# Differential attention: meta rows as one unit, the first softmax's divisor on the outputs, score halves issued alternately

## The chip, the cores and the metric

The kernel runs on one core of one Trainium2 chip. The metric is the device time of one execution in microseconds (us). A core has TensorE (PE, with its weight loads PEld), VectorE (DVE), ScalarE (ACT), GpSimd (POOL) and the queue of SyncE (SP), which work side by side and wait for each other by semaphores. PSUM is the memory that TensorE writes, in 8 banks of 512 fp32 columns.

## The reference, cut to what matters

One encoder layer on two request groups (G = 2) of 512 tokens, each with the same 16 learned meta tokens in front, so T = 528 rows per group. The change touches differential attention alone: 4 heads, each with two halves j of 64 query and key columns and 128 value columns.

```python
def _diff_attention(q, k, v, lam):            # q, k: (B, H, 2, L, 64)
    s = jnp.einsum('bhjqd,bhjkd->bhjqk', qblk, k).astype(jnp.float32)
    p = jax.nn.softmax(s, axis=-1)
    a = p[:, :, 0] - lam * p[:, :, 1]
    return jnp.einsum('bhqk,bhkd->bhqd', a.astype(v.dtype), v)

oa = _diff_attention(dq, dk, dv, lam)
oa = _rmsnorm(oa, g_da_out) * (1.0 - lam_init)   # over the 128 columns of a head
```

Ahead of it stand an RMSNorm and one projection (q, k, v and the mLSTM's inputs); after it the mLSTM, the output projection and 16 experts of expert-choice SwiGLU.

## The kernel before

The program is a row of stages, each a block in which every engine runs its own list: `project`, `attention`, `mlstm`, `project_out`, `experts`. Attention (L677) begins about 400 us into the span and ends at 589.

It works in units (g, c, h): a group, one of five row tiles c (tile 0 holds the 16 meta rows, tiles 1 to 4 hold 128 rows each) and a head, 2 x 5 x 4 = 40 in this order, g outermost. Keys are 528 columns. Meta rows see the keys of their own group, so they are computed once for each group, as 4 units of 16 rows each. The steps of a unit:

- `scores` (L766, TensorE): for each half j, q times k in a split of fp32 into high and low parts (high x high, high x low, low x high), each in two pieces of 264 columns: 12 matmuls, 64 rows deep. Half 0 goes to PSUM banks 0 and 1, half 1 to banks 2 and 3; each half waits for the exponential of the same half of the unit before (`s_exp`), which reads those banks.
- `maxima` (L930, VectorE): the negated maximum of each row and half, from PSUM.
- `softmax` (L831, ScalarE): exp(score - maximum) and its row sum, for each half.
- `combine` (L937, VectorE): the reciprocals of both sums, the second times -lambda, then a = p0 / l0 (L947) and a += p1 x (-lambda / l1) (L948), both 128 x 528.
- `turn` (L782, TensorE) and `read_turned` (L841, ScalarE): a is transposed in five pieces into banks 4 and 5 and copied to SBUF.
- `values` (L793, TensorE): a times v into the head's quarter of bank 6. The first head of a tile waits for `o_read`, that the bank of the tile before has been read.

Four heads make a tile of outputs: `read_out` (L851, ScalarE) copies bank 6 to `osb` (L856) and squares it (L858), `sum_out` (L951, VectorE) adds the squares, `rstd_out` takes the reciprocal root, `norm_out` (L746, POOL) scales by it and by the gain, `turn_out` (L807, TensorE) transposes into bank 7, `store_out` (L865, ScalarE) writes `mixT`.

The order is written out by hand: every engine runs a loop over s, and what it does in turn s is:

```python
# TensorE                                # VectorE
if s < N: scores(s)                      if s < N: maxima(s)
if 2 <= s <= N + 1: turn(s - 2)          if r == 0: sum_out(t)
if 3 <= s <= N + 2: values(s - 3)        if 1 <= s <= N: combine(s - 1)
```

ScalarE's turn s is `store_out` and `read_out` (one turn in four), `rstd_out` (one in four), `softmax(s)`, `read_turned(s - 2)`. In the first turns the engines also split q and k of the next head (`high_qk` on ScalarE, L872 and L873; `low_q` on VectorE, L960; POOL the low part of k, L758), and from turn 4 on, with one step in each of turns 8 to 15, VectorE computes the mLSTM's gate rows (L904 to L927).

Of the kernel before, what the change touches and what calls it, by code (L numbers as in the profile page):

```python
# [676 lines left out]
def attention(nc, e):  # L677
# [13 lines left out]
    rcp = tiles("rcp", [P, 2, 2])  # L691
    so = tiles("so", [P, HEADS])

# [10 lines left out]
    gt_loaded, g_abs, g_exp, l_ready = sem("gt_loaded"), sem("g_abs"), sem("g_exp"), sem("l_ready")  # L704
# [5 lines left out]
    units = [(g, c, h) for g in range(G) for c in range(NC5) for h in range(HEADS)]  # L710
    N = len(units)


    LAST = N + 8

    with nc.Block() as block:

        @block.sync
        def _(sp):
# [9 lines left out]
            load_rows(V, 0, v_loaded)  # L729
            for k in range(4):  # L730
# [12 lines left out]
        def _(pool):  # L743
            step = chained(pool, pool_step)

            def norm_out(t):  # L746
                R = CROWS[t % NC5]
# [3 lines left out]
                o, y = (x[0:R, :].rearrange("p (h d) -> p h d", h=HEADS) for x in (osb, on))  # L751
                step(nc.gpsimd.tensor_tensor(y, o, so[0:R, :].unsqueeze(2).to_broadcast([R, HEADS, HD]), ALU.mult))
                nc.gpsimd.tensor_tensor(y, y, gda[0:R, :].unsqueeze(1).to_broadcast([R, HEADS, HD]),
                                        ALU.mult).then_inc(on_ready, 1)
# [4 lines left out]
            for t in range(G * NC5):  # L759
                norm_out(t)  # L760
# [4 lines left out]
        def _(pe):  # L765
            def scores(i):  # L766
                g, c, h = units[i]
                R, a = CROWS[c], ZCOL[zc(g, c)]
                if i < HEADS:
                    pe.wait_ge(q_low, h + 1)  # L770
                    pe.wait_ge(k_low, h + 1)
                for j in range(2):
                    if i >= 1:
                        pe.wait_ge(s_exp, 2 * (i - 1) + j + 1)
                    for i3, (q, k) in enumerate(((q_hi, k_hi), (q_hi, k_lo), (q_lo, k_hi))):
                        for at, b, end in HALVES:
                            mm = pe.matmul(banks(2 * j, R)[:, at:at + end - b], q[QD * j:QD * j + QD, h, a:a + R],
                                           k[QD * j:QD * j + QD, h, SEQ * g + b:SEQ * g + end], start=(i3 == 0),
                                           stop=(i3 == 2))
                    mm.then_inc(s_done, 1)  # L780

            def turn(i):  # L782
                g, c, _ = units[i]
                R = CROWS[c]
# [3 lines left out]
                for k in range(NC5):  # L788
                    n, b = CROWS[(k + 1) % NC5], kcol(zc(g, (k + 1) % NC5)) - SEQ * g
                    mm = pe.transpose(banks(4, n)[:, k * P:k * P + R], diff[i % 2][0:R, b:b + n], ident[0:R, 0:R])  # L790
                mm.then_inc(aT_done, 1)

            def values(i):  # L793
                g, c, h = units[i]
                R = CROWS[c]
                pe.wait_ge(aT_read, i + 1)
                if c == 0 and h == 0:
                    pe.wait_ge(v_loaded[g], 32 if g == 0 else 16)
                if h == 0 and i > 0:
                    pe.wait_ge(o_read, i // 4)  # L800
                for k in range(NC5):
                    n = P if k < 4 else N_META
                    mm = pe.matmul(banks(6, R)[:, h * HD:(h + 1) * HD], diffT[i % 2][0:n, k, 0:R],
                                   V[0:n, zc(g, (k + 1) % NC5), h * HD:(h + 1) * HD], start=(k == 0), stop=(k == 4))
                mm.then_inc(pv_done, 1)

            def turn_out(t):  # L807
                R = CROWS[t % NC5]
                pe.wait_ge(on_ready, t + 1)
                if t >= 1:  # L810
                    pe.wait_ge(oT_read, t)
                for h in range(HEADS):
                    mm = pe.transpose(banks(7)[:, h * P:h * P + R], on[0:R, h * HD:(h + 1) * HD], ident[0:R, 0:R])
                mm.then_inc(oT_done, 1)

            for s in range(LAST):
# [4 lines left out]
                if 3 <= s <= N + 2:  # L821
                    values(s - 3)
                if s >= 10 and s % 4 == 2 and (s - 10) // 4 < G * NC5:
                    turn_out((s - 10) // 4)

        @block.scalar
        def _(act):
# [3 lines left out]
            def softmax(i):  # L831
                R = CROWS[units[i][1]]
                for j in range(2):
                    act.wait_ge(s_max, 2 * i + j + 1)
                    if i >= 2:
                        act.wait_ge(a_ready, i - 1)
                    nc.scalar.activation(prob[i % 2][j][0:R, :], banks(2 * j, R)[:, PH:PH + T], ACT.Exp,
                                         bias=nmax[0:R, i % 2, j:j + 1],
                                         accum_out=lsum[0:R, i % 2, j:j + 1]).then_inc(s_exp, 1)

            def read_turned(i):  # L841
                R = CROWS[units[i][1]]
                act.wait_ge(aT_done, i + 1)
                if i >= 2:
                    act.wait_ge(pv_done, i - 1)
                src = banks(4)[:, 0:4 * P].rearrange("p (k t) -> p k t", k=4)[:, :, 0:R]
                nc.scalar.activation(diffT[i % 2][:, 0:4, 0:R], src, ACT.Copy)
                nc.scalar.activation(diffT[i % 2][0:N_META, 4, 0:R], banks(5, N_META)[:, 0:R],
                                     ACT.Copy).then_inc(aT_read, 1)

            def read_out(t):  # L851
                R = CROWS[t % NC5]
                act.wait_ge(pv_done, 4 * t + 4)
                if t >= 1:
                    act.wait_ge(on_ready, t)
                nc.scalar.activation(osb[0:R, :], banks(6, R)[:, 0:HALF], ACT.Copy).then_inc(o_read, 1)  # L856
                act.wait_ge(o_read, t + 1)
                nc.scalar.activation(osq[0:R, :], osb[0:R, :], ACT.Square).then_inc(osq_ready, 1)  # L858

            def rstd_out(t):  # L860
                R = CROWS[t % NC5]
                act.wait_ge(so_ready, t + 1)
                rms_rstd(nc, step, so[0:R, :], so[0:R, :], HD, eps[0:R, :]).then_inc(or_ready, 1)

            def store_out(t):  # L865
                R, a = CROWS[t % NC5], mixcol(*divmod(t, NC5))
                act.wait_ge(oT_done, t + 1)
                src = banks(7)[:, 0:HALF].rearrange("p (h t) -> p h t", h=HEADS)[:, :, 0:R]
                nc.scalar.activation(mixT[:, 0:HEADS, a:a + R], src, ACT.Copy).then_inc(oT_read, 1)
# [4 lines left out]

            high_qk(0)
            high_qk(1)
            for s in range(LAST + 2):
                t, r = divmod(s - 7, 4)
                if r == 0 and 0 <= t - 1 < G * NC5:
                    store_out(t - 1)  # L880
                if r == 0 and 0 <= t < G * NC5:
                    read_out(t)
                if r == 1 and 0 <= t < G * NC5:
                    rstd_out(t)
                if 2 <= s + 1 < HEADS:
                    high_qk(s + 1)
                if s < N:
                    softmax(s)
                if 2 <= s <= N + 1:
                    read_turned(s - 2)  # L890
                if s == 5:
# [3 lines left out]
                    nc.scalar.activation(ga[:], ga[:], ACT.Ln, bias=1.0).then_inc(g_exp, 1)  # L895

        @block.vector
        def _(dve):
# [31 lines left out]
            def maxima(i):  # L930
                R = CROWS[units[i][1]]
                for j in range(2):
                    dve.wait_ge(s_done, 2 * i + j + 1)
                    nc.vector.tensor_reduce(nmax[0:R, i % 2, j:j + 1], banks(2 * j, R)[:, PH:PH + T], AX.X, ALU.max,
                                            negate=True).then_inc(s_max, 1)

            def combine(i):  # L937

                R = CROWS[units[i][1]]
                dve.wait_ge(s_exp, 2 * i + 2)  # L940
                r = rcp[0:R, i % 2]
                step(nc.vector.reciprocal(r, lsum[0:R, i % 2]))
# [1088 lines left out]
```

## Time and profile before

| | us |
|---|---|
| median of 3 runs | 2556.29 |
| lowest and highest | 2554.6, 2564.03 |
| the profiled execution | 2560.51 |
| its span, first to last instruction | 2558.7 |
| of it the attention stage, first splitting to last store | 400.5 to 589.1 |
| busy over the whole span: PE, DVE, ACT, POOL | 94%, 76%, 66%, 10% |
| busy in 400.30 to 589.10: PE, DVE, ACT, POOL | 157.7, 147.0, 110.2, 36.0 |
| TensorE's granted clock, whole span, and in 400.30 to 589.10 | 0.96, 0.82 |

The profiled execution lies 4.2 us above the median. 1.00 of the granted clock is 2.4 GHz and 0.50 is 1.2 GHz; a number between is a mean over a stretch. Idle time is named in brackets in the rows, with what ended it. A matmul of fp32 operands appears as two records where it isn't a transpose, so the five products of `values` are ten.

### The profile page before, as it was taken

The page shows a single profiled execution, that of the slowest core. Times are in us where ns is not written, and L with a number is a line of the kernel's source. Part 1 is how long each engine was busy: PE and PEld are TensorE (multiplying, and loading weights), DVE is VectorE, ACT ScalarE, POOL GpSimd, SP SyncE. Part 2 cuts the span into 40 slices and gives each one's busy share as a digit, 9 for nine tenths or more (in the row PEclk, how much of TensorE's full clock was granted, in tenths as well). Part 3 has the DMA queues.
Part 4 walks back from the last instruction along what each step waited for, and adds up shares of the span by engine and source line. Part 5 has one row for each costly group of instructions (what it writes and reads, how often), then busy time and mean ns, then how long its engine had stood idle before and what let it go on. Part 6 is the DMA issues. An engine that isn't in the chain of part 4 may idle for free.

```text
span 2558.7 us, 51699 instructions
## 1 busy us (share of the span) xinstructions
PE 2412.1 (94%) x21830; PEld 2206.4 (86%) x21830; DVE 1934.0 (76%) x2311; ACT 1697.3 (66%) x2379; POOL 265.6 (10%) x174
## 2 busy tenths in 40 slices
PE   7999997998979929999999999999999999999997
PEld 5777884785757729999999999999999999999997
DVE  4621035884873359999998998998999999989986
ACT  7311224573443228888888888887888888888885
POOL 3312111110122010000000000000000000000000
PEclk9999996896889959999999999999999999999999
DMA  4122101001023359999999999999999999999993
GB/s 124 33 86 81 66 17 35 1 13 56 1 91 123 116 187 321 366 362 349 366 360 350 381 346 352 379 344 366 366 349 365 362 348 368 360 348 383 345 365 127
DMA packets 325114, 624.33 MB, mean 244 GB/s; under 512 B 11828, under 2 KB 48788, under 8 KB 324884
## 3 DMA queue, kind: packets, MB, share of 16 engines
q1 hardware_dynamic: 317220, 602.78, 66.2%
q0 software_dynamic: 7664, 18.25, 3.6%
q8 instruction: 173, 2.83, 0.5%
q14 instruction: 57, 0.47, 0.1%
HBM read 597.23 MB, written 23.69 MB: 243 GB/s over the span
## 4 chain that ended last, share of the span: by engine, by line
PE 59%; issue 3%; DVE 1%; DMA 1%; POOL 0%; ACT 0%; POOLq 0%
PE ps L1750 26%; PE ps L1778 13%; PE ps L1756 13%; PE ps L1784 6%; PE ps L1795 1%; PE ps L1732 1%; POOL xg L1693 0%; DMA xg<-xn_rows,idxT 0%; DVE vals L1924 0%; DVE index L1927 0%; DMA out_rows<-yr,idxT 0%; DVE aff L1926 0%; POOL out_rows L1701 0%; POOLq L1672 0%; PE ps L1716 0%
## 5 line engine op out<-in xcount | busy, mean ns | idle before, releaser
L1916 DVE TENSOR_TENSOR wlo<-raw,whi 128x2048 bf16<-128x2048 f32 (+1 forms) x436 | 963.6, 2223 | 55.0 <-ACT whi L1822 55.0
L1822 ACT ACTIVATE whi<-raw 128x2048 fp32r<-128x2048 f32 (+1 forms) x436 | 804.9, 1859 | 37.6 <-PE ps L1784 37.6
L1750 PE MATMUL ps<-xx,whi 128*128 128x264 f32 x4512 | 616.2, 289 | 3.6 <-DVE xx L1967 3.6
L1750 PEld LDWEIGHTS ps<-xx,whi 128*128 128x128 f32 x4512 | 564.2, 189 | 3.8 <-DVE xx L1967 3.8
L1756 PE MATMUL ps<-xb,wlo 128*128 128x132 bf16 x4512 | 313.7, 221 | 0.0
L1778 PE MATMUL ps<-hx,whi 128*128 128x264 f32 x2256 | 312.3, 290 | 0.0
L1778 PEld LDWEIGHTS ps<-hx,whi 128*128 128x128 f32 x2256 | 283.8, 189 | 0.0
L1756 PEld LDWEIGHTS ps<-xb,wlo 128*128 128x128 bf16 x4512 | 264.0, 97 | 13.8
L1916 DVE TENSOR_TENSOR wlo_last<-raw,whi_last 128x2048 bf16<-128x2048 f32 (+1 forms) x108 | 240.5, 2227 | 13.6 <-ACT whi_last L1822 13.6
L1832 ACT ACTIVATE low<-ps 128x264 f32<-128x264 f32 x352 | 137.7, 391 | 135.7 <-PE ps L1756 122.0
L1822 ACT ACTIVATE whi_last<-raw 128x2048 fp32r<-128x2048 f32 (+1 forms) x108 | 201.5, 1866 | 9.3 <-PE ps L1784 9.3
L1701 POOL DMA_INDIRECT out_rows<-yr,idxT x32 | 48.4, 1512 | 1235.8 <-ACT yr L1877 1231.0
L1784 PE MATMUL ps<-hb,wlo 128*128 128x132 bf16 x2256 | 157.0, 221 | 0.0
L1750 PE MATMUL ps<-xx,whi_last 128*128 128x264 f32 x1120 | 154.1, 290 | 0.0
L444 PE MATMUL ps<-w_hi,h_hi 128*128 128x512 f32 (+1 forms) x360 | 144.3, 401 | 4.5 <-POOL w_lo L314 4.5
L444 PE MATMUL ps<-w_hi,h_lo 128*128 128x512 f32 (+1 forms) x360 | 141.6, 393 | 0.0
L444 PE MATMUL ps<-w_lo,h_hi 128*128 128x512 f32 (+1 forms) x360 | 141.6, 393 | 0.0
L1750 PEld LDWEIGHTS ps<-xx,whi_last 128*128 128x128 f32 x1120 | 141.2, 189 | 0.0
L1784 PEld LDWEIGHTS ps<-hb,wlo 128*128 128x128 bf16 x2256 | 130.1, 98 | 7.7
L1945 DVE TENSOR_TENSOR gs<-ps,low 128x264 f32<-128x264 f32 x176 | 74.9, 426 | 30.7 <-ACT low L1832 30.7
L522 ACT ACTIVATE w_hi<-w 128x1024 fp32r<-128x1024 f32 x28 | 29.4, 1054 | 103.5 <-DMA w<-in_w_in 103.5
L671 DVE TENSOR_SCALAR cy<-zp,cols 128x1056 f32<-128x1056 f32 x8 | 6.2, 770 | 120.8 <-ACT zp L581 120.8
(236 smaller groups left out, 3463.4 us busy)
## 6 DMA issues: line engine op xcount, KB each, us to landing
raw<-in_w_gate SPq DMA_DIRECT2D x80, 2048.0 KB, 12.7
raw<-in_w_up SPq DMA_DIRECT2D x80, 2048.0 KB, 10.3
raw<-in_w_down SPq DMA_DIRECT2D x64, 2048.0 KB, 10.7
raw<-in_w_down SPq DMA_DIRECT2D x32, 1536.0 KB, 8.1
raw<-in_w_gate SPq DMA_DIRECT2D x16, 1024.0 KB, 9.0
raw<-in_w_up SPq DMA_DIRECT2D x16, 1024.0 KB, 11.6
w<-in_w_in SPq DMA_DIRECT2D x28, 512.0 KB, 4.9
zv_rows<-qn SPq DMA_DIRECT2D x24, 256.0 KB, 2.0
```

Source lines behind the costliest of these rows:

```text
L444: mm = pe.matmul(banks(4 + i % 3, ZROWS[c])[:, 0:512], h, w, start=(k == 0 and i3 == 0), stop=(k == KD - 1 and i3 == 2))
L522: nc.scalar.activation(w_hi[u % NW][:], w_whole[u % NW][:], ACT.Copy).then_inc(w_high, 1)
L1701: nc.gpsimd.indirect_dma_start(out, bass.IndirectOffsetOnAxis(ap=idxT[:, g, ex:ex + 1], axis=0), yr[:, g, :], None, compute_op=ALU.add).th ...
L1732: mm = pe.transpose(banks(b)[:, at:at + CAP], xg[:, g, k * P:(k + 1) * P], ident[0:CAP, 0:CAP])
L1750: pe.matmul(banks(b + i)[:, 0:2 * C2], w[:, k, i * P:(i + 1) * P], xx[:, k], start=(k == 0), stop=False, skip_group_check=True)
L1756: mm = pe.matmul(banks(b + i)[:, 0:C2], w[:, k, i * P:(i + 1) * P], xb[:, k], start=False, stop=(k == KD - 1), skip_group_check=True)
L1778: pe.matmul(banks(b + i)[:, 0:2 * C2], w[:, c, i * P:(i + 1) * P], hx[:, c0 + c], start=(c0 + c == 0), stop=False, skip_group_check=True)
L1784: mm = pe.matmul(banks(b + i)[:, 0:C2], w[:, c, i * P:(i + 1) * P], hb[:, c0 + c], start=False, stop=(c0 + c == M - 1), skip_group_check=True)
L1822: nc.scalar.activation(shaped(whi[n % R_SPLIT], u), unit_raw(raw, ex, u), ACT.Copy).then_inc(hi_ready, 1)
L1832: nc.scalar.activation(low[u % 2][:], src, ACT.Copy).then_inc(low_ready, 1)
L1916: nc.vector.tensor_tensor(shaped(wlo[n % R_SPLIT], u), unit_raw(raw, ex, u), shaped(whi[n % R_SPLIT], u).bitcast(F32), ALU.subtract).then_ ...
L1945: nc.vector.tensor_tensor((gs, us)[kind][:], src, low[kind][:], ALU.add).then_inc(sum_ready, 1)
```

## The change

Three things are changed in `attention`, and nothing elsewhere.

1. The eight units of meta rows become one, META = 20, in the middle of the order; the other 32 units are whole tiles of 128 rows, so N is 33. Its 128 rows are 16 rows for each of 8 pairs (group, head), at `cell(g, h)`. Its queries stand in zero-padded tiles `zq_hi` and `zq_lo`, so that the scores of all 8 pairs add up in the same banks without mixing: 8 x 12 = 96 matmuls in `scores(META)`. `turn` takes each group's keys for its 64 rows (10 matmuls with an identity in place of 5 transposes), `values_meta` makes 40 matmuls of 16 columns into bank 7, and the norm of these columns goes by its own small steps (`square_meta`, `sum_meta`, `rstd_meta`, `store_meta`).
2. In the other units a isn't divided by l0: `combine` forms p0 + p1 x (-lambda x l0 / l1) in one pass, keeps 1/l0 of each head in `r0`, and `read_out`, now on VectorE, multiplies the outputs by it while it reads bank 6. ScalarE keeps the square (`square_out`).
3. `scores` issues the two halves alternately, and waits at its head for both exponentials of the unit before.

The places of the outputs' steps are tables now: READ is the last unit of the tile + 4, SUM + 5, TURN + 7.

```diff
+    META = 20
+    N = HEADS * len(TILES) + 1
+    READ = {last(t) + 4: t for t in range(len(TILES))}
+    SUM = {last(t) + 5: t for t in range(len(TILES))}
+    TURN = {last(t) + 7: t for t in range(len(TILES))}
...
             def scores(i):
...
-                for j in range(2):
-                    if i >= 1:
-                        pe.wait_ge(s_exp, 2 * (i - 1) + j + 1)
-                    for i3, (q, k) in enumerate(((q_hi, k_hi), (q_hi, k_lo), (q_lo, k_hi))):
+                if i >= 1:
+                    pe.wait_ge(s_exp, 2 * i)
+                if i == META:
+                    pe.wait_ge(zq_ready, 1)
+                    parts = [(zq_hi[:, h, 64 * (1 - g):64 * (1 - g) + P], zq_lo[:, h, 64 * (1 - g):64 * (1 - g) + P], g, h)
+                             for g in range(G) for h in range(HEADS)]
+                else:
...
+                    parts = [(q_hi[:, h, a:a + P], q_lo[:, h, a:a + P], g, h)]
+                for n, (qh, ql, g, h) in enumerate(parts):
+                    for i3, (q, k) in enumerate(((qh, k_hi), (qh, k_lo), (ql, k_hi))):
                         for at, b, end in HALVES:
...
+                            for j in range(2):
+                                rows = slice(QD * j, QD * j + QD)
+                                mm = pe.matmul(banks(2 * j)[:, at:at + end - b], q[rows],
+                                               k[rows, h, SEQ * g + b:SEQ * g + end], start=(n == 0 and i3 == 0),
+                                               stop=(n == len(parts) - 1 and i3 == 2))
...
             def combine(i):
...
-                step(nc.vector.tensor_scalar(diff[i % 2][0:R, :], p0, r[:, 0:1], None, ALU.mult))
-                nc.vector.scalar_tensor_tensor(diff[i % 2][0:R, :], p1, r[:, 1:2], diff[i % 2][0:R, :], ALU.mult,
-                                               ALU.add).then_inc(a_ready, 1)
...
+                    step(nc.vector.reciprocal(r, l))
+                    nc.vector.tensor_copy(r0[:, t % 2, h:h + 1], r[:, 0:1])
+                    step(nc.vector.scalar_tensor_tensor(r[:, 1:2], r[:, 1:2], lam[:, 3:4], l[:, 0:1], ALU.mult, ALU.mult))
+                    if i >= 2:
+                        dve.wait_ge(aT_done, i - 1)
+                    nc.vector.scalar_tensor_tensor(diff[i % 2][:], p1, r[:, 1:2], p0, ALU.mult, ALU.add).then_inc(a_ready, 1)
+
+            def read_out(t):
+                dve.wait_ge(pv_done, HEADS * (t + 1))
+                if t >= 1:
+                    dve.wait_ge(on_ready, t)
+                src, dst = (x.rearrange("p (h d) -> p h d", h=HEADS) for x in (banks(6)[:, 0:HALF], osb[:]))
+                nc.vector.tensor_tensor(dst, src, r0[:, t % 2].unsqueeze(2).to_broadcast([P, HEADS, HD]),
+                                        ALU.mult).then_inc(o_read, 1)
...
+            def values_meta():
+                pe.wait_ge(aT_read, META + 1)
+                pe.wait_ge(oT_read, BEFORE_META)
...
+                for g in range(G):
+                    for h in range(HEADS):
+                        a = cell(g, h)
+                        for k in range(NC5):
+                            n = P if k < 4 else N_META
+                            mm = pe.matmul(banks(7)[:, a:a + N_META], V[0:n, zc(g, (k + 1) % NC5), h * HD:(h + 1) * HD],
+                                           diffT[META % 2][0:n, k, a:a + N_META], start=(k == 0), stop=(k == 4))
+                mm.then_inc(meta_out, 1)
...
                 if s < N:
                     maxima(s)
...
+                if s in SUM:
+                    sum_out(SUM[s])
                 if 1 <= s <= N:
                     combine(s - 1)
+                if s in READ:
+                    read_out(READ[s])
```

On POOL, two memsets of the zero-padded tiles (128 x 768) and one of ones follow the splitting of k; SP loads the gain as a column (`gcol`) behind the loads of V; ScalarE copies the 16 meta columns of q into the padded tiles in turn 8 (`spread_meta`).

VectorE before, in a turn in which ScalarE reads the outputs (nmax are the maxima, rcp the reciprocals, diff is a, so the sums of squares):

```order
L934 TENSOR_REDUCE nmax<-ps 128x1 [waits s_done] x2
L954 TENSOR_REDUCE so<-osq 128x4 [waits osq_ready]
L942 RECIPROCAL rcp<-lsum 128x2 [waits s_exp]
L943 TENSOR_TENSOR rcp<-rcp,lam 128x1 [waits dve_step]
L947 TENSOR_SCALAR diff_3193<-prob_3189,rcp 128x528 [waits aT_done,dve_step]
L948 SCALAR_TENSOR_TENSOR diff_3193<-prob_3190,rcp,diff_3193 128x528 [waits dve_step]
```

VectorE now, in turn 28, a READ turn, and the head of the next:

```order
L1025 TENSOR_REDUCE nmax<-ps 128x1 [waits s_done] x2
L1042 RECIPROCAL rcp<-lsum 128x2 [waits s_exp]
L1043 COPY r_3203<-rcp 128x1 [waits dve_step]
L1044 SCALAR_TENSOR_TENSOR rcp<-rcp,lam,lsum 128x1
L1047 SCALAR_TENSOR_TENSOR diff_3194<-prob_3192,rcp,prob_3191 128x528 [waits aT_done,dve_step]
L1054 TENSOR_TENSOR osb<-ps,r_3203 128x512 [waits on_ready,pv_done]
L1025 TENSOR_REDUCE nmax<-ps 128x1 [waits s_done] x2
L1059 TENSOR_REDUCE so<-osq 128x4 [waits osq_ready]
```

L947 is gone, a one-column copy is new, and the reading of the outputs stands behind the turn's combination. TensorE in the same kind of turn, before:

```order
L777 MATMUL ps<-k_hi,q_hi 128x264 [waits s_exp]
L777 MATMUL ps<-k_hi,q_hi 128x264
L777 MATMUL ps<-kT_lo,q_hi 128x264 x2
L777 MATMUL ps<-k_hi,qT_lo 128x264 x2
L777 MATMUL ps<-k_hi,q_hi 128x264 [waits s_exp]
L777 MATMUL ps<-k_hi,q_hi 128x264
L777 MATMUL ps<-kT_lo,q_hi 128x264 x2
L777 MATMUL ps<-k_hi,qT_lo 128x264 x2
L790 MATMUL ps<-ident,diff_3194 128x128 [waits aT_read,a_ready]
L790 MATMUL ps<-ident,diff_3194 128x128 x3
L790 MATMUL ps<-ident,diff_3194 16x128
L803 MATMUL ps<-V,diffT_3195 128x128 [waits o_read,aT_read]
```

And now, in turn 28:

```order
L820 MATMUL ps<-k_hi,q_hi 128x264 [waits s_exp]
L820 MATMUL ps<-k_hi,q_hi 128x264 x3
L820 MATMUL ps<-kT_lo,q_hi 128x264 x4
L820 MATMUL ps<-k_hi,qT_lo 128x264 x4
L840 MATMUL ps<-ident,diff_3193 128x128 [waits aT_read,a_ready]
L840 MATMUL ps<-ident,diff_3193 128x128 x3
L840 MATMUL ps<-ident,diff_3193 16x128
L853 MATMUL ps<-V,diffT_3196 128x128 [waits o_read,aT_read]
```

The twelve score matmuls have one wait in place of two; the wait for `o_read` stands at the same place, and what releases it has moved from ScalarE's queue to VectorE's. In the order of before the meta units stand where the tile index is 0, with the same rows at 16 in place of 128 and at L803 as `16x128`.

## Rows read from the trace of the kernel before

**Rows 1.** Windows by clock; clock is the seventh column, after the engines' busy time

```profile
433.34:448.00 14.66, 14.66 (x74) 10.99 (x74) 9.60 (x19) 8.20 (x19) 0.00 (x0) 0.50 0.01 2
448.00:471.90 23.90, 21.39 (x166) 18.72 (x166) 22.23 (x40) 13.34 (x41) 5.49 (x4) 1.00 0.00 1
471.90:499.30 27.40, 25.84 (x148) 22.65 (x147) 22.20 (x41) 14.78 (x41) 3.23 (x2) 0.69 0.01 1
499.30:571.40 72.10, 70.12 (x585) 58.12 (x584) 62.63 (x127) 51.26 (x148) 12.04 (x10) 1.00 0.00 1
```

**Rows 2.** Timeline, one slot with the clock up: start us, us, engine, line, operation

```profile
551.75 0.51 PE L777 MATMUL ps<-k_hi,q_hi 64*128 64x264 f32 x2
...
552.11 0.38 PE L777 MATMUL ps<-k_hi,q_hi 64*128 64x264 f32 x1
...
552.22 0.28 PE L777 MATMUL ps<-kT_lo,q_hi 64*128 64x264 f32 x1
...
552.78 1.32 DVE L934 TENSOR_REDUCE nmax<-ps 128x1 f32<-128x528 f32 x2 [0.26 <-PE ps L777]
...
553.02 0.77 PE L790 MATMUL ps<-ident,diff 128*128 128x128 f32 x5
...
553.53 0.70 ACT L837 ACTIVATE prob<-ps,nmax 128x528 f32<-128x528 f32 x1 [1.09 <-DVE nmax L934]
...
553.62 1.47 PE L803 MATMUL ps<-V,diffT 128*128 128x128 f32 x10
...
555.02 0.65 PE L813 MATMUL ps<-ident,on 128*128 128x128 f32 x4
```

**Rows 3.** Timeline, two slots with gate work on VectorE

```profile
468.12 1.32 DVE L934 TENSOR_REDUCE nmax<-ps 128x1 f32<-128x528 f32 x2
...
468.87 0.70 ACT L837 ACTIVATE prob<-ps,nmax 128x528 f32<-128x528 f32 x1 [3.04 <-DVE nmax L934]
...
469.56 0.69 ACT L837 ACTIVATE prob<-ps,nmax 128x528 f32<-128x528 f32 x1
...
469.71 0.50 PE L777 MATMUL ps<-k_hi,q_hi 64*128 64x264 f32 x2 [1.50 <-ACT prob L837]
...
470.96 1.24 DVE L920 TENSOR_TENSOR_SCAN rowt<-gb,ga 8x528 f32<-8x528 f32 x1
...
472.24 1.32 DVE L934 TENSOR_REDUCE nmax<-ps 128x1 f32<-128x528 f32 x2
```

**Rows 4.** Lines of the combination on VectorE: ns least, median, most

```profile
L943 DVE TENSOR_TENSOR rcp<-rcp,lam x40: 147/159/931, 416.4 to 574.3; 128x1 f32<-128x1 f32 x32, 16x1 f32<-16x1 f32 x8
...
L947 DVE TENSOR_SCALAR diff<-prob,rcp x40: 481/495/1583, 416.6 to 575.2; 128x528 f32<-128x528 f32 x32, 16x528 f32<-16x528 f32 x8
```

**Rows 5.** Timeline where outputs are read, and a two-operand read of PSUM

```profile
570.28 0.59 ACT L856 ACTIVATE osb<-ps 128x512 f32<-128x512 f32 x1
...
571.55 1.47 PE L803 MATMUL ps<-V,diffT 128*128 128x128 f32 x10
...
L1532 DVE TENSOR_TENSOR x<-ps,xr x9: 1212/1224/1225, 777.8 to 884.3; 128x1024 f32<-128x1024 f32 x8, 32x1024 f32<-32x1024 f32 x1
```

**Rows 6.** Timeline of TensorE, one slot with the clock down

```profile
438.48 0.81 PE L777 MATMUL ps<-k_hi,q_hi 64*128 64x264 f32 x2
...
439.10 0.58 PE L777 MATMUL ps<-k_hi,q_hi 64*128 64x264 f32 x1
...
444.32 0.81 PE L777 MATMUL ps<-k_hi,q_hi 64*128 64x264 f32 x2
```

**Rows 7.** Timeline, the third unit's first exponential

```profile
422.34 0.69 ACT L837 ACTIVATE prob<-ps,nmax 16x528 f32<-16x528 f32 x1 [3.24 <-DVE nmax L934]
```

**Rows 8.** Timeline: turning of 16 rows, and the stage's end

```profile
511.79 0.44 PE L790 MATMUL ps<-ident,diff 16*128 16x16 f32 x5
...
578.21 2.97 PE L803 MATMUL ps<-V,diffT 128*128 128x128 f32 x20
...
588.50 0.60 ACT L869 ACTIVATE mixT<-ps 128x512 f32<-128x512 f32 x1 [3.66 <-PE ps L813]
```

More of the change, by code:

```diff
@@ L708, in attention, with unit, normal, last @@
     q_high, q_low, k_high, k_low = (sem(s) for s in "q_high q_low k_high k_low".split())
-    units = [(g, c, h) for g in range(G) for c in range(NC5) for h in range(HEADS)]
-    N = len(units)
+    TILES = [(g, c) for g in range(G) for c in range(1, NC5)]
+    META = 20
+    N = HEADS * len(TILES) + 1
+    def unit(i):
+        return divmod(i - (1 if i > META else 0), HEADS)
+    def normal(i):
+        return i - (1 if i > META else 0)
+    def last(t):
+        i = HEADS * t + HEADS - 1
+        return i + (1 if i >= META else 0)
+    READ = {last(t) + 4: t for t in range(len(TILES))}
+    SUM = {last(t) + 5: t for t in range(len(TILES))}
+    TURN = {last(t) + 7: t for t in range(len(TILES))}
     LAST = N + 8
+    BEFORE_META = sum(s < META + 3 for s in TURN)
+    def cell(g, h):
+        return N_META * (HEADS * g + h)
     with nc.Block() as block:
@@ L758, in _ @@
                 nc.gpsimd.tensor_tensor(k_lo[:, h], kT[:, h], k_hi[:, h].bitcast(F32), ALU.subtract).then_inc(k_low, 1)
-            for t in range(G * NC5):
+            nc.gpsimd.memset(ones[:], 1.0).then_inc(zero_made, 1)
+            for z in (zq_hi, zq_lo):
+                nc.gpsimd.memset(z[:].bitcast(F32), 0.0).then_inc(zero_made, 1)
+            for t in range(len(TILES)):
                 norm_out(t)
@@ L788, in turn @@
                 for k in range(NC5):
-                    n, b = CROWS[(k + 1) % NC5], kcol(zc(g, (k + 1) % NC5)) - SEQ * g
-                    mm = pe.transpose(banks(4, n)[:, k * P:k * P + R], diff[i % 2][0:R, b:b + n], ident[0:R, 0:R])
+                    n = CROWS[(k + 1) % NC5]
+                    at = [kcol(zc(g, (k + 1) % NC5)) - SEQ * g for g in range(G)]
+                    if i == META:
+                        for g in range(G):
+                            half = slice(64 * g, 64 * g + 64)
+                            mm = pe.matmul(banks(4, n)[:, k * P + 64 * g:k * P + 64 * g + 64], diff[i % 2][:, at[g]:at[g] + n],
+                                           ident[:, half], start=True, stop=True)
+                    else:
+                        b = at[TILES[unit(i)[0]][0]]
+                        mm = pe.transpose(banks(4, n)[:, k * P:(k + 1) * P], diff[i % 2][:, b:b + n], ident[:])
@@ L807, in turn_out, with sum_meta @@
+            def sum_meta():
+                pe.wait_ge(zero_made, 3)
+                pe.wait_ge(meta_out, META_SQUARES)
+                pe.matmul(banks(7)[:, P:2 * P], ones[:], sqm[:], start=True, stop=True).then_inc(meta_out, 1)
             def turn_out(t):
-                R = CROWS[t % NC5]
                 pe.wait_ge(on_ready, t + 1)
@@ L831, in softmax @@
             def softmax(i):
-                R = CROWS[units[i][1]]
                 for j in range(2):
@@ L940, in combine @@
                 dve.wait_ge(s_exp, 2 * i + 2)
[L941 to L949 removed]
+                r, l = rcp[:, i % 2], lsum[:, i % 2]
```

178 lines of the change are left out of this document (110 added, 68 removed).

## The prediction

> **What bounds the kernel now.** I read the page's slices first: TensorE is busy nearly everywhere, but the attention stage (400 to 589 us) is the one place that this change touches, 7% of the span. Then the stretches by clock [rows 1]: TensorE's granted clock was at its lower level (1.2 GHz, 0.50) from 433 to 448 us, at the higher (2.4 GHz) until 471.9, 0.69 in the mean from 471.9 to 499.3 (so 62% of those 27.4 us, 17.0 us, were down), and up from 499.3 on. Of the 138 us from 433.3 to 571.4, 14.7 + 17.0 = 31.7 us, 23%, were down. Then the timeline, slot by slot. A slot is one turn of the TensorE queue: scores of unit s, turning of s-2, values of s-3.
>
> With the clock up, TensorE fills the slot [rows 2]: 1.27 us scores (551.75 to 553.02), 0.60 turning, 1.40 values, 3.27 in all, and 0.59 more in every fourth slot for turning the outputs. VectorE is close behind: two maxima and a combination take 472.24 - 468.12 = 4.12 us with a gate step of 1.24 between them, so 2.88 without [rows 3]. With the clock down a slot is 5.84 us, all TensorE [rows 6].
>
> The two halves already overlap [rows 2]: program order is six matmuls of half 0, then six of half 1, yet half 1 starts at 552.11, 0.36 us after half 0, and before a later matmul of half 0 (552.22). Each half goes on at one matmul per 0.12 us.
>
> **The change, part by part.** I write the time from one slot's first score matmul to the next one's.
>
> *Alternate halves.* TensorE saves the lag of half 1: 0.36 us with the clock up, 439.10 - 438.48 = 0.62 down [rows 2, 6]. So its slot becomes 2.91 and 5.2. But scores(i) now waits for both exponentials of i-1, where half 0 used to wait for the first alone. That closes a ring: scores to maxima 1.03, to the first exponential 0.75 [rows 2], two exponentials 2 x 0.69, and 0.14 from its end (468.87 + 0.70) to the waiting matmul [rows 3]: 1.03 + 0.75 + 1.38 + 0.14 = **3.30 us**. With the clock up this ring, not TensorE's 2.91, sets a plain slot, about what it was. Here the Trainium skill ("TensorE: Matmul & The Clock Gate", Part 3, The mechanism) says matmuls start and end strictly in program order and that only neighbours in different row groups run together. By that rule the old halves would not overlap, alternating would save 0.70 us a slot up and 1.3 down, and my sum would be some 5 us lower. The row at 552.11 contradicts it, and the row decides.
>
> *Divisor moved to the outputs.* VectorE loses the scaling of 0.50 [rows 4] with its 0.03 gap and gains a one-column copy, which the trace lacks; it lies between nothing and the 0.50 of a whole row, nearest the one-column product's 0.16 [rows 4], which I take. So maxima and combination take 2.5. The product with V is now read out of PSUM by VectorE, which applies the divisor. The nearest row is a two-operand read of PSUM with 1024 columns, 1.22 [rows 5], so 0.65 for 512; the bounds are the old 0.59 on ScalarE and 0.8.
>
> *What is queued behind it.* The read of tile t stands in VectorE's queue behind maxima(s) and combine(s-1), and TensorE's values of the next tile's first head, in that same slot s, wait for it, since they reuse the bank. Before, ScalarE read it at 570.28, ahead of its exponentials, and values started at 571.55 unheld [rows 5]. Now: maxima start at 1.03, the combination ends at 3.5, the read at 4.2, values take 1.4: a **held slot of 5.7 us**, in which TensorE stands still from about 1.5 to 4.2. It happens in six slots (7, 11, 15, 19, 28, 32); in slot 23 the order puts the meta unit's values there instead. ScalarE's square waits too, but its own slack covers that.
>
> *Units.* Forty units become 33. The first four were meta units that cost start-up time, not work: exponentials 1 and 2 follow the splitting of the next heads' q and k on ScalarE, POOL and VectorE [rows 7], which stays. So scores(3) starts near 422.34 + 1.38 + 0.14 = 423.9, slots 3 and 4 take 5.3 with the clock down, and slot 5 starts at 434.5. From there, with the clock up:
> - 8 plain slots x 3.3 = 26.4; 2 with outputs turned (2.91 + 0.59) = 7.0; 6 held x 5.7 = 34.2
> - 7 slots with gate work on VectorE: 27.4. Six have 2.5 + 1.24 [rows 3], one of them 0.3 shorter, and two with the sum of squares 0.66 more, half of a pair of maxima's 1.32 [rows 2]: 23.5. Slot 5 has three gate steps, which start in the shadow of its cold start: 3.9
> - the meta unit: its scores are 96 matmuls, 48 pairs x 0.117 = 5.6 for 0.7, slot 8.2. Its turning is 20 passes, its values 80 passes with 16 columns. The nearest row is five passes of 16 columns in 0.44, 0.067 each once the 0.17 of the last one's own length is off [rows 8]; the upper bound is 0.14, values' own 1.40 / 10 [rows 2]. I take 0.067, since 16 columns stream: slots of 4.3 and 7.0 (12.8 at the upper bound). The small sum and the outputs turned behind its store (4.6) with it: 27.5 in all.
>
> That is 122.5 us: scores end at 557.0. The tail is 5.4 for what is left on TensorE, then the old 8.0 from values' end (578.21 + 2.97) to the last store (589.1) [rows 8], less 1.2 that now lies elsewhere: 569.2. **Clock up throughout: 19.9 us less.** The memsets, the gain column's small load and the spreading of q stand where POOL, SP and ScalarE idle; without that cover they cost 1 to 2 us once.
>
> *The clock.* After a TensorE wait of 1.50 us at 469.71 the clock fell at 471.9 [rows 1, 3], and the stretch to 499.3 holds 17.0 us down in two falls, 8.5 each. The six held slots have 2.7 us of standing each. Down, plain slots cost 5.2 (and turning outputs 1.1 more), held ones 7.3 (maxima start at 1.7 in place of 1.03, and values take twice 1.2), the meta slots near double (15.0, 7.8, 13.5, and 6.3 for the store): 16 x 5.2 + 4 x 1.1 + 2 x 5.2 + 6 x 7.3 + 42.6 = 184.4 for the 122.5, so a microsecond down does 0.66 of the work. Six falls of about 7 us are 30% of the stretch: 122.5 / (1 - 0.34 x 0.30) = 136.4, 13.9 us back. Sum: -19.9 + 13.9 = **-6 us** on the profiled execution's 2560.5 (span 2558.7); it lies 4.2 above the median of the runs, 2556.3, so I forecast **2550 us**.
>
> **The rivals.** A measurement of this kernel tells about 0.5%, 12.8 us, from no change.
> - *The clock hardly falls.* For it: all tiles are now whole, and from 499.3 to 571.4 the clock never fell. Against: the held slots stand longer than any wait there. Down under 17% of the time, the gain passes 12.8; with none it is 19.9: 2536. Chance 0.24.
> - *The read does not hold values* (or by far less). Then six times 2.4, 14 more, is gained and the pauses go too: -34, 2522. Against: the order rows show the wait and the queue. Chance 0.06.
> - *The alternate issue does nothing*, since the array overlapped the halves already. With the clock up that costs nothing in my sum (3.27 is under 3.30); down it is 0.6 in some eight slots, 5 us: 2555. It lies in the forecast's case.
> - *Slower: the clock stays down behind the held slots.* TensorE's only full stretches are the meta unit and the slots between pauses. All down is 184.4 - 122.5 = 62 us over the sum, +42: 2598. It decides when more than 62% of the stretch is down: 122.5 / (1 - 0.34 x 0.62) = 155.2, +12.8. For it: from 433 to 448 us TensorE was busy throughout at the lower clock. Against: those slots had small tiles. Chance 0.13.
>
> **The numbers.** The forecast's case (17 to 62% down) has 0.57, faster by over 0.5% 0.30 (two rivals), slower 0.13. The range goes from 2533 (no fall, a cheaper read) to 2568 (60% down, or the meta passes at their upper bound, +6, with 40% down).
>
> **What would show it.** Right: plain slots near 3.3 us with TensorE waiting for the exponential; VectorE's read ending 4.2 us after the slot's first score and values idle until then in six slots; the meta unit's scores near 5.6 us, its values 5 to 6; the clock down again after held slots; the last store near 583. Wrong: values unheld, plain slots of 3.0, or a clock that is up (or down) all the way. Behind the stage nothing is touched, so the gain should be carried to the end whole, but for a few us where the mLSTM's own clock falls differently.

## The result, and the profile after

| | before | after |
|---|---|---|
| median of 4 runs each, us | 2558.97 | 2569.94 |
| lowest and highest | 2554.6, 2564.03 | 2568.81, 2571.23 |
| the profiled execution, and its span | 2560.51, 2558.7 | 2568.81, 2567.0 |
| last attention store ends at | 589.1 | 597.2 |

The ratio of after to before is 1.0043, with a 95% interval of 1.0025 to 1.0061: slower by 11 us between the medians, where 6 us less was forecast. The range ended at 2568. The two profiled executions lie 8.3 us apart, and all of that but 0.2 arises in attention: its last store ends 8.1 us later, and the stretch of the mLSTM behind it takes the same (589.1 to 700.0 before, 597.2 to 708.0 after).

First the held slots. What TensorE waited for in the whole stage of the changed kernel, its start-up included, by line (us in total, times, longest):

```profile
PE ps L820 <- ACT prob L910: 17.8, 10, 5.0
PE ps L853 <- DVE osb L1054: 15.9, 6, 2.9
```

The second line is the wait that the prediction set up: six times, on VectorE's reading of the outputs. One of them in the timeline, with the plain slot ahead of it:

```profile
558.42 0.70 ACT L910 ACTIVATE prob<-ps,nmax 128x528 f32<-128x528 f32 x1 [1.07 <-DVE nmax L1025]
...
559.95 0.51 PE L820 MATMUL ps<-k_hi,q_hi 64*128 64x264 f32 x4 [0.31 <-ACT prob L910]
...
560.98 1.32 DVE L1025 TENSOR_REDUCE nmax<-ps 128x1 f32<-128x528 f32 x2 [0.79 <-PE ps L820]
...
561.72 0.70 ACT L910 ACTIVATE prob<-ps,nmax 128x528 f32<-128x528 f32 x1 [1.21 <-DVE nmax L1025]
...
562.72 0.77 DVE L1047 SCALAR_TENSOR_TENSOR diff<-prob,rcp,prob 128x528 f32<-128x528 f32 x1
...
563.41 0.68 DVE L1054 TENSOR_TENSOR osb<-ps,r 128x512 f32<-128x512 f32 x1
...
564.24 2.58 PE L853 MATMUL ps<-V,diffT 128*128 128x128 f32 x10 [2.60 <-DVE osb L1054]
...
566.75 0.81 PE L820 MATMUL ps<-k_hi,q_hi 64*128 64x264 f32 x4
```

The read ends 4.14 us after the slot's first score matmul (forecast 4.2) and TensorE stands for 2.60. Values then took 2.58, where unheld ones took 1.47 [rows 2, 5], since the clock fell at 564.4: the slot is 6.80 us, not 5.7. Of the first line of the waits only 5.1 us lie behind the start-up: four stands of 0.3 us are the ring, and two of 2.17 and 1.68 us come behind slots with gate work. Plain slots between exponentials measure 3.30 (558.42 to 561.72), as worked out.

Then the meta unit, by its own rows:

```profile
508.32 0.64 PE L820 MATMUL ps<-k_hi,zq_hi 64*128 64x264 f32 x4
...
511.20 0.41 PE L820 MATMUL ps<-k_hi,zq_hi 64*128 64x264 f32 x4
...
520.33 2.33 PE L836 MATMUL ps<-ident,diff 128*128 128x64 f32 x20 [0.19 <-DVE diff L1038]
...
526.20 15.47 PE L867 MATMUL ps<-diffT,V 128*128 128x16 f32 x80
526.44 0.70 ACT L910 ACTIVATE prob<-ps,nmax 128x528 f32<-128x528 f32 x1 [1.06 <-DVE nmax L1025]
...
541.60 0.81 PE L820 MATMUL ps<-k_hi,q_hi 64*128 64x264 f32 x4
541.71 0.28 ACT L956 ACTIVATE sqm<-ps 128x128 f32<-128x128 f32 x1 [11.48 <-PE ps L867]
...
544.06 0.70 ACT L910 ACTIVATE prob<-ps,nmax 128x528 f32<-128x528 f32 x1 [2.08 <-DVE nmax L1025]
```

Its values run from 526.20 to 541.60, **15.4 us for 80 passes, where 5.4 was forecast**; the next unit's scores stand behind them in TensorE's queue, and ScalarE and VectorE behind those (ScalarE was idle for 11.48 us). From one exponential to the next is 17.62 us. The clock, by stretches:

```profile
434.50:584.20 149.70, 127.20 (x931) 110.01 (x929) 89.53 (x196) 72.89 (x208) 17.07 (x12) 0.81 0.02 5
526.20:541.60 15.40, 15.40 (x82) 14.86 (x81) 2.54 (x7) 2.74 (x7) 0.00 (x0) 0.63 0.01 2
```

A mean of 0.81 means that 38% of the stretch was down (30% forecast). The clock went down eight times, at 438.1, 445.0, 468.9, 479.1, 489.3, 506.4, 530.3 and 564.4. Five of these falls came within a wait for the read or some 2 us behind it. Those at 438.1 and 479.1 came some 1 us behind the waits of 2.17 and 1.68 us for an exponential. The fall at 530.3 came in the middle of the meta unit's values, with TensorE busy all 15.40 us, and lasted until 550.8. The stage ends so:

```profile
596.58 0.60 ACT L936 ACTIVATE mixT<-ps 128x512 f32<-128x512 f32 x1 [3.66 <-PE ps L883]
```

### The profile page after: what moved, and what is told of

Its sections match the earlier page's. It is cut to its first block, busy times and chain, and to the rows that moved or that the text cites. A ratio compares the mean times of both kernels' runs of the same rounds, so it can differ in the third digit from the quotient of the medians.

```text
span 2567.0 us, 51528 instructions
## 1 busy us (share of the span) xinstructions
PE 2402.1 (94%) x21804; PEld 2204.6 (86%) x21804; DVE 1903.6 (74%) x2277; ACT 1681.8 (66%) x2331; POOL 264.0 (10%) x173
## 4 chain that ended last, share of the span: by engine, by line
PE 59%; issue 3%; DVE 1%; DMA 1%; POOL 0%; ACT 0%; POOLq 0%
PE ps L1867 26%; PE ps L1895 13%; PE ps L1873 12%; PE ps L1901 6%; PE ps L1912 1%; PE ps L1849 1%; DMA xg<-xn_rows,idxT 0%; POOL xg L1810 0%; DVE vals L2041 0%; DVE index L2044 0%; DMA out_rows<-yr,idxT 0%; DVE aff L2043 0%; POOL out_rows L1818 0%; POOLq L1789 0%; PE ps L1833 0%
```

## The experiments

Each was timed in five rounds beside the kernel before, whose medians in the three series were 2556.77, 2556.65 and 2556.36 us. Ratios are to that kernel. The theory at the outset: two losses, the six held slots and the meta unit's narrow passes, and falls of the clock that both bring.

**1. The read ahead of the maxima.** The read needs nothing of its turn, so its place in VectorE's queue alone holds it.

```diff
+                if s in READ:
+                    read_out(READ[s])
                 if s < N:
                     maxima(s)
...
                     combine(s - 1)
-                if s in READ:
-                    read_out(READ[s])
```

> The changed kernel with one move: VectorE reads a tile's outputs ahead of the turn's maxima, not behind its combination. Theory H (held slots): values are no longer held for 2.6 us in six slots, so 15.9 us of waiting go, and some falls of the clock behind them; 15 to 25 us less than the changed kernel, 2545 to 2555 us, and below the kernel before. Theory M (the meta unit's values are what made the kernel slower, the held slots are paid for by the clock and the ring anyway): 5 us or less.

Measured: 2548.93 us, ratio 0.9963 (0.9949 to 0.9976), 21.0 under the changed kernel by the medians. The wait of L853 is gone from the view of waits. The stage from 434.5 to the last store, first in the changed kernel, then here (window, its length, busy times; then the clock, 0.82 and 0.88):

```profile
434.50:597.20 162.70, 134.59 (x979) 115.88 (x977) 91.94 (x200) 77.01 (x218) 22.20 (x17) 0.82 0.09 27
434.50:577.10 142.60, 123.36 (x987) 106.33 (x985) 94.02 (x200) 76.17 (x218) 22.16 (x17) 0.88 0.10 31
```

That is 20.1 us less. The waits were 15.9 us; the rest goes with the clock, up from 0.82 to 0.88. So two lines of order turn the change from a loss of 0.4% into a gain of 0.4%.

**2. The meta unit's values cut to a fifth.** One key tile of five is left in; the other four fifths of the meta rows' keys are left out.

```diff
-                        for k in range(NC5):
+                        for k in range(1):
...
-                                           diffT[META % 2][0:n, k, a:a + N_META], start=(k == 0), stop=(k == 4))
+                                           diffT[META % 2][0:n, k, a:a + N_META], start=(k == 0), stop=(k == 0))
```

> The changed kernel whose meta unit makes only the first of five products for each of its 8 outputs (8 matmuls in place of 40), so its meta rows leave out four fifths of the keys. Theory M: 64 of 80 passes go. At 0.125 us each with the clock up and 0.24 down they took 15.5 us in all, so 12 us go, and the fall of the clock at 530.3 (20.5 us down) may go as well, 3 to 5 us more: 2553 to 2558 us. Theory H: the queues behind it give little of it back as gain, 5 us or less, since VectorE and ScalarE need their time for the same units: 2565.

Measured: 2555.8 us, 0.9992 (0.9982 to 1.0001), 14.1 under the changed kernel. The slot of the meta values fell from 17.62 to 3.85 us, and the long stretch at the lower clock under it went with them; the six held slots stayed.

**3. Both together.**

> The kernel with the read moved ahead of the maxima (2548.9 us), and in addition only 8 of the meta unit's 40 score and value products (four fifths of the keys of that unit are left out; the rest is computed as before). My theory: the meta unit's narrow passes, and the stretch at the lower clock under them, are the second loss beside the held slots and stand in the chain by themselves, so the slot of its values falls from 17.3 us to about 4 and the time by 12 to 16 us: 2533 to 2537 us. Rival: with the held slots gone TensorE has room, and the narrow passes are mostly hidden: a gain of 5 us or less, 2544 us or more.

Measured: 2530.94 us, 0.9901 (0.9886 to 0.9916): 18.0 under experiment 1, a little more than expected. The slot fell from 17.31 to 3.31, 14.0 us, and the clock was up nearly throughout. TensorE's meta values in it, and the stage:

```profile
512.21 1.86 PE L867 MATMUL ps<-diffT,V 128*128 128x16 f32 x16
```

```profile
434.50:559.60 125.10, 103.47 (x923) 87.11 (x922) 94.21 (x200) 75.69 (x218) 22.16 (x17) 0.97 0.11 35
```

The remaining 4 us go with falls of the clock that experiment 1 had and this run did not: some 2.3 us ahead of the part that was edited (falls at 457 and 474, and a longer one at 440), and 1.6 behind it (a fall at 563). Why the earlier ones stayed away is open. Held slots (0.80% of the time by the ratios) and meta values (0.51%) add up to 1.31%, both at once gave 1.42%: the two losses are nearly independent, and the rival, that TensorE's room hides the narrow passes once it isn't held, is out.

**4. The halves in their old order, in the changed kernel.**

```diff
-                if i >= 1:
-                    pe.wait_ge(s_exp, 2 * i)
...
-                for n, (qh, ql, g, h) in enumerate(parts):
-                    for i3, (q, k) in enumerate(((qh, k_hi), (qh, k_lo), (ql, k_hi))):
-                        for at, b, end in HALVES:
-                            for j in range(2):
+                for j in range(2):
+                    if i >= 1:
+                        pe.wait_ge(s_exp, 2 * (i - 1) + j + 1)
+                    for n, (qh, ql, g, h) in enumerate(parts):
+                        for i3, (q, k) in enumerate(((qh, k_hi), (qh, k_lo), (ql, k_hi))):
+                            for at, b, end in HALVES:
```

> The changed kernel with the old issue order: six matmuls of half 0, then six of half 1, each half behind its own exponential. The ring theory: alternate issue frees 0.36 us (0.62 with the clock down) of TensorE but closes the ring of 3.30 us; with the old order a plain slot is set by TensorE at 3.27, and slots with the clock down are 0.6 longer. With 39% of the stretch down that is 5 us more at most, 2570 to 2576. The skill's program-order rule: the halves would not overlap, 0.7 us a slot more, 20 us and more over 33 slots plus 5 us in the meta unit: 2590 or above.

Measured: 2591.84 us, 1.0133 (1.0115 to 1.0150), 21.9 over the changed kernel: a miss for my expectation, and in the rival's range (2590 or above). But the loss is not where the rival put most of it: plain slots with the clock up are 3.28 us, not 0.7 longer. The meta unit's scores in it:

```profile
509.55 0.64 PE L820 MATMUL ps<-k_hi,zq_hi 64*128 64x264 f32 x2
509.99 0.64 PE L820 MATMUL ps<-kT_lo,zq_hi 64*128 64x264 f32 x2
510.43 0.64 PE L820 MATMUL ps<-k_hi,zq_lo 64*128 64x264 f32 x2
```

Two matmuls take 0.44 us here, and in the changed kernel at the same clock four do (508.32 above). With 48 matmuls of one half in a row the halves run one behind the other. In experiment 5, which has the same order, only the seam between the two runs shows them side by side, for some 0.5 us (the second line is the other half's first matmul):

```profile
498.90 0.28 PE L820 MATMUL ps<-kT_lo,zq_hi 64*128 64x264 f32 x1
498.91 0.38 PE L820 MATMUL ps<-k_hi,zq_hi 64*128 64x264 f32 x1
```

The slots from unit 19 to 21 take 16.18 + 13.74 us in place of 12.38 + 3.30, 14.2 more. Not all of this is the order: the clock was down from 506.9 to 530.8 here, and for 3.4 us of the same slots in the changed kernel. The order costs 5.0 us there with the clock up (experiment 5); down, by an estimate from the 0.22 us of a matmul above, 48 x 0.22 = 10.6. The other 7.7 us of the 21.9 are not assigned slot by slot. The Trainium skill ("TensorE: Matmul & The Clock Gate", Part 3, The mechanism) has the rule that matmuls start and end in program order and overlap only across row groups. In runs of 48 it holds but for the seam; in runs of six the row at 552.11 [rows 2] and the plain slots of the next experiment speak against any such cost.

**5. The same with the read first.**

> Both moves: outputs read first, and the old issue order. If the ring is what is left once values aren't held, this is at or below the first of these runs, by up to 3 us where the clock is up; if TensorE is what is left, it is 3 to 8 us above it.

Measured: 2556.28 us, 0.9992 (0.9982 to 1.0002), 7.3 over experiment 1, as expected if TensorE is what is left; but that is so in the meta unit above all, not in the plain slots. Plain slots are 3.27 to 3.28 against 3.30, slots with outputs turned 3.87 against 3.51, the meta unit 8.37 + 8.36 against 8.40 + 3.29. So the alternate issue is worth 5.0 us in the meta unit and 0.36 where TensorE has more to do, and costs 0.03 in a plain slot.

**6. The alternate issue alone, in the kernel before.**

```diff
-                for j in range(2):
-                    if i >= 1:
-                        pe.wait_ge(s_exp, 2 * (i - 1) + j + 1)
...
+                if i >= 1:
+                    pe.wait_ge(s_exp, 2 * i)
...
+                        for j in range(2):
```

> The kernel before with one part of the change: scores issues the two halves alternately and waits for both exponentials. Ring theory: a plain slot goes from 3.27 (TensorE) to the ring's 3.30, the slot with outputs turned from 3.85 to 3.6, slots with the clock down lose 0.6: -5 to +2 us against the kernel before. Rival (alternate issue alone is worth the 22 us that undoing it cost in the changed kernel): 2535 to 2545.

Measured: 2553.88 us, 0.9989 (0.9980 to 0.9999): 2.8 less, its slots 3.30.

**7. The divisor alone, read first, in the kernel before.** The combination in one pass, `read_out` on VectorE ahead of the maxima, forty units, old issue order.

> The kernel before with the first softmax's divisor moved to the outputs alone, the read issued ahead of the maxima; the two halves in their old order and forty units. My theory: the plain slots stay at 3.27 us, since TensorE fills them in the old order and does not wait for the read; the slots with a gate lose the divisor's passes on VectorE and fall from 4.11 us to some 3.75: 3 to 8 us less than before, 2549 to 2554 us. Rival: the values wait for a later read in the old order too: no gain or a loss, 2557 us or more.

Measured: 2548.32 us, 0.9964 (0.9952 to 0.9976): 8.0 less. Slots with a gate step fell from 4.11 to 3.70, where 3.75 was expected.

**8. Both, with forty units** (edits 6 and 7 together).

> The kernel before with alternate issue and the divisor on the outputs, read by VectorE ahead of the maxima, but the 40 units as they were: the read-first kernel without the meta unit. If merging the meta rows is worth what seven units fewer promise (7 x 3.3 = 23 us), this is 20 us above the read-first kernel's 2549. If the meta unit's 96 score matmuls, its 20 and its 80 narrow passes eat it, the two lie within 5 us: the meta unit took 5.1 + 2.2 + 14.0 = 21 us over plain slots there.

Measured: 2546.04 us, 0.9957 (0.9944 to 0.9971). This is the fastest of the complete versions and beats both kernels, 10.6 under before and 23.9 under the changed one; experiments 1 and 7 lie within its interval. Merging the meta rows therefore brings nothing over forty units. The slots say why: merged (experiment 1), the unit takes 8.40 for scores, 5.52 in its turning slot and 17.31 in its values slot, 21.3 more than three plain slots, and 1.3 more in the slot of its small sum (4.63), and saves seven slots of 3.3, 23.

**9. Forty units, the read late.** Experiment 8 with the read in the change's place, behind the combination of the unit before; the square follows the softmax and its sum comes one turn later.

```diff
-                if r == 0 and 0 <= t < G * NC5:
-                    read_out(t)
                 if s < N:
                     maxima(s)
...
                     combine(s - 1)
+                if r == 0 and 0 <= t < G * NC5:
+                    read_out(t)
```

> The version with forty units (no merged meta unit), alternate issue and the divisor moved (2546.0 us with the read ahead of the maxima), but with the read in the change's place: behind the combination of the unit before, so that the values wait for it. My theory: a held slot costs 2.4 us and lets the clock fall behind it whether or not the meta rows are merged; eight or nine such slots are 20 us and some falls of the clock that come with them, 2562 to 2572 us. Rival: the held slots cost only together with the merged meta unit, since the plain slots have room to take them in: 5 us or less, at most 2551 us.

Measured: 2581.4 us, 1.0097 (1.0082 to 1.0113), 35.4 over experiment 8, more than expected. Its waits, its stage and the same stage of experiment 8:

```profile
PE ps L805 <- DVE osb L954: 23.5, 9, 3.0
```

```profile
433.00:609.70 176.70, 141.70 (x1014) 113.29 (x1013) 111.15 (x244) 89.56 (x256) 27.25 (x21) 0.80 0.08 25
```

```profile
433.00:573.80 140.80, 121.35 (x1030) 97.71 (x1028) 115.39 (x246) 89.03 (x260) 25.06 (x21) 0.94 0.10 31
```

Nine held slots are 23.5 us of standing, 2.6 each; the remaining 12 go with the clock, 0.80 against 0.94. So a held slot costs with or without the meta unit, about 3.9 us with its share of the clock; in the changed kernel 21.0 / 6 = 3.5.

**10. The meta unit last** (experiment 1 with META = 32).

> The read-first kernel with the meta unit as the last of the 33 in place of the 21st. Its products then run while TensorE has nothing but the end of the last tile's outputs to wait for (6 us of waiting in the read-first kernel's tail). If that cover holds: 5 to 8 us less than read-first, 2541 to 2544. If the tail becomes the meta unit's own chain of products, squares, sum and store, no gain, or up to 5 us more.

Measured: 2549.48 us, 0.9972 (0.9962 to 0.9983): the same as experiment 1 within the intervals. The last exponential comes at 543.4 in place of 559.9, but the unit's own chain makes the tail: the clock is down from 550.2 on, and the 80 passes, wholly at the lower level, take 18.87 us.

**11. More work for TensorE in the pause.** The changed kernel, with 12 matmuls into unused columns of bank 7 ahead of the wait for the read, in five held slots.

```diff
+                if h == 0 and 0 < t < 7 and i - 1 != META:
+                    if t > 1:
+                        pe.wait_ge(oT_read, t - 1)
+                    for _ in range(12):
+                        pe.matmul(banks(7)[:, P:512], q_hi[:, 0, 0:P], k_hi[:, 0, 0:512 - P], start=True, stop=True)
                 if h == 0 and t > 0:
                     pe.wait_ge(o_read, t)
```

> The changed kernel with 12 matmuls of 384 columns (1.9 us with the clock up, 3.9 down, into unused columns) ahead of the wait for the outputs' read in five of the six held slots. They do no part of the computation. If the clock falls because TensorE stands still in the held slots, the falls there go and the run is 3 to 8 us faster than the changed kernel, 2562 to 2567, though TensorE does more work. If the clock's falls have another cause, it is 0 to 8 us slower, since a filler that runs with the clock down outlasts the pause.

Measured: 2562.73 us, 1.0018 (1.0008 to 1.0027): **7.2 us less with more work**. Its stage to the last store (the changed kernel's is shown at experiment 1):

```profile
434.50:592.20 157.70, 137.03 (x1059) 118.80 (x1059) 94.65 (x202) 77.34 (x220) 22.15 (x17) 0.88 0.09 28
```

TensorE is busy 137.03 of 157.7 us where it was busy 134.59 of 162.7, and its clock is up for more of the time, 0.88 against 0.82. The held slots stay (their slots 5.7 to 6.2, the forecast's 5.7). The falls behind the five that were filled are all gone, one comes behind the sixth, which was not filled (574.2), and the fall under the meta values (526.4 to 543.5) stays. So the pause causes the falls behind held slots, and something else the one under the narrow passes; what that is, no run isolates.

## Why the prediction was wrong

**Right: the ring.** "With the clock up this ring, not TensorE's 2.91, sets a plain slot": 3.30 forecast, 3.30 measured in every version with the alternate issue, and 3.27 in the old order.

**Right: the held slots**, in the place, number (six) and length (read ended 4.14 against 4.2; the read itself 0.68 against 0.65, the combination's single pass 0.77). They were in the sum, at 34.2 us. What I made nothing of is that they were avoidable, and enough to turn the sign: without them the change is 7.8 us faster than before (experiment 1).

**The step that failed: the price of the meta unit's passes.** "I take 0.067, since 16 columns stream: slots of 4.3 and 7.0 (12.8 at the upper bound)." The row behind it [rows 8] is a transposition of the same shape, one record for each piece. A product of fp32 operands is two, and each costs more: a pass cost what a full one costs. Short stretches show the step from one record to the next; the length of the last one itself has to come off. From the kernel before, then from the changed one:

```profile
553.73 0.94 PE L803 MATMUL ps<-V,diffT 128*128 128x128 f32 x7
515.94 0.71 PE L803 MATMUL ps<-V,diffT 128*16 128x128 f32 x5
```

```profile
526.34 0.71 PE L867 MATMUL ps<-diffT,V 128*128 128x16 f32 x5
532.63 1.23 PE L867 MATMUL ps<-diffT,V 128*128 128x16 f32 x5
520.49 1.73 PE L836 MATMUL ps<-ident,diff 128*128 128x64 f32 x14
522.26 0.40 PE L836 MATMUL ps<-ident,diff 128*16 128x64 f32 x4
```

The pair ahead of the second shape is the loaded operand (rows * columns), the second shape the moving one. With 128 loaded columns a record takes (0.94 - 0.27) / 6 = 0.11 us when 128 columns move, (1.73 - 0.28) / 13 = 0.11 when 64 move and (0.71 - 0.26) / 4 = 0.11 when 16 move, and (1.23 - 0.37) / 4 = 0.21 after the fall of the clock. So the count of columns that stream does not cheapen it at all. The last line, four records of the same line and the same 64 moving columns with 16 loaded ones, gives (0.40 - 0.22) / 3 = 0.06: the loaded columns set the price there. Exchanging the operands would not help, since 16 loaded and 128 moving columns take (0.71 - 0.27) / 4 = 0.11. The price goes with the larger of the two counts in these rows; no experiment varied them. Two passes of every ten have 16 rows, and the changes to and from them cost more; so the mean over all 80 was 0.125 until 530.3 (33 records) and 0.24 from there on (47).

The Trainium skill ("TensorE: Matmul & The Clock Gate", Part 2, LDWEIGHTS) gives 107 ns for a load of 128 columns, whatever the rows. The trace agrees at the upper clock for these products (0.11); at the lower one it has 0.21, and the transpositions of 16 rows, which load 128 columns too, follow each other in 0.06 to 0.07 [rows 8], so the figure does not cover those.

The upper bound of 0.14 stood in the prediction, the mean of ten passes of the same line kind, two of them with 16 rows; the nearest in shape was taken, and the nearest in operation was right.

**And the clock under them.** I counted six falls, all behind held slots, "30% of the stretch". Five came behind held slots, two behind waits for an exponential, and an eighth inside the meta values, with TensorE busy throughout. What the passes and the clock do to my own formula: the passes at 0.125 add 4.6 to the values and 1.2 to the turning, and 122.5 becomes 128.3. The clock was down for 58.0 us of the 151.9 from slot 5's start (432.4) to the end of slot 32 (584.3), 38%: 128.3 / (1 - 0.34 x 0.38) = 147.3 us. The forecast was 136.4, and the slots took 151.9. So 10.9 of the 15.5 us are found: 6.5 by the passes alone at 30%, 4.4 by the clock. Of the other 4.6 some 1.5 are the meta values again, in which a microsecond down does half the work (0.11 against 0.21) and not 0.66; the last 3 I cannot assign. Slot 5 had started 2.1 us ahead of the forecast 434.5, since the clock was up from 427.9; with that, the last store came 14 us behind the forecast 583.1.

**The rivals.** "The alternate issue does nothing" holds for plain slots, but not in the meta unit, where old order costs 5 us (experiments 4 and 5), which no rival had. "The clock hardly falls" had 0.24 and "the read does not hold values" 0.06; both are refuted for this kernel. Their numbers were too low as well, for the passes were missing in them: with the read unheld I had put 2522, and experiment 1 gave 2549; a clock that was up nearly throughout came only with the read unheld and four fifths of the meta values gone (experiment 3, 2531). The slower rival decided at 62% down; the time went up with 38% down, since the passes joined it. I had named that combination for the end of the range ("the meta passes at their upper bound, +6, with 40% down", 2568), but my own formula does not give 2568 for it: 128.5 / (1 - 0.34 x 0.40) = 148.7 is 6.3 us over the kernel before, 2562.6. Only 60% down gives 2568. So the combination that came, at 2569.9, had been priced some 7 us too low, and its chance was undersized.

## What to carry to other kernels

When a reading of PSUM moves to another engine, put it ahead of everything in that engine's turn that doesn't feed it: here its place in the queue decided 21 us of 2557. Before small units are merged into one with many narrow matmuls, price each pass from a row of the same operation (not of a transposition): here passes with 16 moving columns cost the same 0.11 us as those with 128. If TensorE must stand between busy stretches, add the lower clock behind the pause to the price of the pause.

## What the runs showed of the hardware

- A record of an fp32 product with 128 loaded columns took 0.11 us with the clock up, whether 16, 64 or 128 columns moved, and 0.21 with it down (16 moving); with 16 loaded and 64 moving columns it took 0.06, with 16 loaded and 128 moving 0.11.
- The granted clock fell from 2.4 to 1.2 GHz during 16-column passes although the profile shows no idle time on TensorE, in the changed kernel (530.3), in experiment 1 (518.6) and in experiment 11 (526.4); with a fifth of the passes it did not. Twelve useless matmuls in each of five pauses made the kernel 7.2 us faster.
- Halves in different row groups overlap in their old order when each has six matmuls (0.36 us between their starts). When each has 48 they do so only at the seam: with the clock down two took 0.44 us, and four took the same when alternated.
